# A mixture-of-experts decoder step: one weight transfer per expert instead of two, and the down product right behind its own activations

## The reference, cut to what matters

```python
def _swiglu(x, wg, wu, wd):
    return (jax.nn.silu(x @ wg) * (x @ wu)) @ wd

def block_fn(args):
    toks, e = args
    xb = xf[toks]
    return _swiglu(xb, w_gate[e], w_up[e], w_down[e])

yb = lax.map(block_fn, (row_tok.reshape(n_blocks, EXPERT_BLOCK), block_e))
return jax.ops.segment_sum(yb.reshape(R, D) * row_w[:, None], row_tok, num_segments=N)
```

## Time and profile before

| | us |
|---|---|
| median of 3 runs (lowest, highest) | 2084.97 (2083.36, 2092.01) |
| the profiled execution's own time | 2083.33 |
| its span, first to last instruction | 2081.7 |

### The profile page before, as it was taken

One profiled execution on the slowest core, in us unless ns is written; L12 is line 12 of the kernel. 1 busy time (PEld: TensorE's weight loads), 2 busy tenths in 40 slices (PEclk: granted clock), 3 DMA queues, 4 the chain that ended last, 5 costly groups with the idle time before them and its releaser, 6 DMA issues. The chain is left out here.

```text
span 2081.7 us, 34017 instructions
## 1 busy us (share of the span) xinstructions
PE 1714.9 (82%) x13065; PEld 1021.8 (49%) x13066; DVE 703.9 (34%) x1821; ACT 311.1 (15%) x665; POOL 355.2 (17%) x453
## 2 busy tenths in 40 slices
PE   5997988488889998785699988986688999987875
PEld 3455655244455454443355666654344555544432
DVE  0211235511413432231711265547312333331226
ACT  0221201110001111001002244331001111110110
POOL 3000100122212222221001011100122222222220
PEclk8999999699899999998789999998799999998997
DMA  9479874699999999994922599995499999999966
GB/s 329 169 264 348 313 303 138 268 416 425 393 383 370 421 418 407 401 401 180 350 105 71 189 291 329 326 343 216 195 423 420 397 409 403 421 411 401 402 278 227
DMA packets 132060, 674.14 MB, mean 324 GB/s; under 512 B 28111, under 2 KB 40527, under 8 KB 91620
## 3 DMA queue, kind: packets, MB, share of 16 engines
q1 hardware_dynamic: 84880, 570.20, 69.6%
q10 hardware_dynamic: 21604, 55.96, 8.0%
q0 software_dynamic: 25456, 46.27, 6.2%
HBM read 651.03 MB, written 46.94 MB: 335 GB/s over the span
## 5 line engine op out<-in xcount | busy, mean ns | idle before, releaser
L2323 PE MATMUL bank<-ring,work 128*64 128x256 f32 x4096 | 535.8, 420 | 145.6 <-DMA ring<-in_exp_w 143.2
L2323 PEld LDWEIGHTS bank<-ring,work 128*64 128x64 f32 x4096 | 341.7, 151 | 309.0 <-issue 130.6
L2051 PE MATMUL bank<-ring,uT 128*128 128x512 f32 (+1 forms) x896 | 253.7, 498 | 5.5 <-DVE u L1481 4.2
L2335 PE MATMUL bank<-ring,work 128*64 128x512 f32 x1032 | 249.9, 605 | 1.3 <-DVE work L1762 0.9
L811 POOL DMA_INDIRECT work<-u_d,work x128 | 130.6, 1021 | 641.7 <-DVE work L1728 352.7
L1728 DVE COPY work<-work 128x1 int32<-128x1 int32 (+1 forms) x128 | 19.2, 153 | 530.1 <-ACT work L1184 529.3
L2051 PEld LDWEIGHTS bank<-ring,uT 128*128 128x128 f32 (+1 forms) x896 | 117.6, 167 | 132.1 <-issue 112.0
L818 POOL DMA_INDIRECT pair_d<-work x128 | 132.6, 1036 | 268.1 <-DVE work L1732 255.1
L1184 ACT ACTIVATE work<-bank 128x128 f32<-128x128 f32 x128 | 35.5, 277 | 675.9 <-PE bank L2323 675.9
L1180 ACT COPY work<-bank 128x512 f32<-128x512 f32 x128 | 74.9, 585 | 292.8 <-PE bank L2335 292.8
L2315 PE MATMUL bank<-ident,work 128*128 128x128 f32 x516 | 97.5, 312 | 20.2 <-DMA work<-u_d,work 20.2
(11 more groups left out here) (363 smaller groups left out, 1735.9 us busy)
## 6 DMA issues: line engine op xcount, KB each, us to landing
ring<-in_exp_w SPq DMA_DIRECT2D x128, 2048.0 KB, 17.8
ring<-in_exp_w SPq DMA_DIRECT2D x128, 1024.0 KB, 13.0
ring<-in_ada_w SPq DMA_DIRECT2D x24, 2048.0 KB, 11.7
ring<-in_cache_k SPq DMA_DIRECT2D x128, 256.0 KB, 6.6
ring<-in_cache_v SPq DMA_DIRECT2D x128, 256.0 KB, 6.8
ring<-in_gla_w_in SPq DMA_DIRECT2D x6, 2048.0 KB, 18.1
ring<-in_kv_w_mod SPq DMA_DIRECT2D x4, 2048.0 KB, 11.7
work<-pair_d ACTq DMA_DIRECT2D x4, 2048.0 KB, 9.6
```

Source lines behind the costliest of these rows:

```text
L2051: ins = mm(out, uT[:, c, t0:t0 + r], ring_pair(unit)[:, c, cols], start=(c == 0), stop=(c == KT - 1), skip_group_check=(t == ST))
L2323: ins = mm(psum[s][64 * c:64 * c + 64, 0:2 * P].rearrange("p (a n) -> p a n", a=2), xT[:, s, j * P + 64 * half:j * P + 64 * half + 64], gu ...
L2335: ins = mm(psum[3 + s][64 * c:64 * c + 64, :], hT[:, s, 64 * f:64 * f + 64], w[:, f, c * 512:(c + 1) * 512], start=(f == 0), stop=(f == 1) ...
```

## The change

Each expert's 3 MB come as one transfer with runs of 24 KB in each partition, issued when the down product of expert e-3 is finished; one semaphore per slot tells of all three matrices. On TensorE the down product of expert e directly follows the transpose of its own hidden values, still behind the transposes of the rows of expert e+1. On DVE the copy of the hidden values goes ahead of the copy of the turned rows. On ACT the copy of the result of e-1 goes ahead of the `silu` of e. The separate down product behind the loop goes.

```diff
             def moe(l):
                 wr.at(0)
                 for e in range(NE):
-                    wr.take(("gate_up", l, e), 2, (h_full, NE * l + e + 1))
-                    wr.take(("down", l, e), 1, (y_full, NE * l + e + 1))
+                    wr.take(("expert", l, e), 3, (y_full, NE * l + e + 1))
...
             def load_expert(l, e, s):
 
-                sp.dma_start(ring[:, 3 * s:3 * s + 2, :].rearrange("p a n -> p (a n)"),
-                             W["exp_w"][l, ds(e, 1)].rearrange("o p n -> p (o n)")[:, 0:2 * UNIT])\
-                  .then_inc(unit_full[3 * s], 16)
-
-            def load_down(l, e, s):
-                sp.dma_start(ring[:, 3 * s + 2, :],
-                             W["exp_w"][l, ds(e, 1)].rearrange("o p n -> p (o n)")[:, 2 * UNIT:3 * UNIT])\
-                  .then_inc(unit_full[3 * s + 2], 16)
+                sp.dma_start(ring[:, 3 * s:3 * s + 3, :].rearrange("p a n -> p (a n)"),
+                             W["exp_w"][l, ds(e, 1)].rearrange("o p n -> p (o n)")).then_inc(unit_full[3 * s], 16)
 
             def load_experts(l):
                 for e in range(3):
-                    free_units(("gate_up", l, e))
+                    free_units(("expert", l, e))
                     load_expert(l, e, e)
-                    free_units(("down", l, e))
-                    load_down(l, e, e)
                 base = l * NE
                 load_shared(l)
 
                 def steady(e, s):
-                    sp.wait_ge(h_full, e + (base - 2))
+                    sp.wait_ge(y_full, e + (base - 2))
                     load_expert(l, e, s)
-                    sp.wait_ge(y_full, e + (base - 2))
-                    load_down(l, e, s)
...
                 def one(e, s, i, first=False):
+                    if not first:
+                        y_out(e - 1, (s + 2) % 3, stored_before(e - 1, (s + 2) % 3, i))
                     act.wait_ge(h_full, e + (base + 1))
                     act.activation(sil[:, s, :], psum[s][:, 0:P], ACT.Silu).then_inc(sem("sil_ready"), 1)
-                    if not first:
-                        y_out(e - 1, (s + 2) % 3, stored_before(e - 1, (s + 2) % 3, i))
...
                     tt(hs[:, s, :], sil[:, s, :], psum[s][:, P:2 * P], ALU.mult).then_inc(sem("h_ready"), 1)
+                    dve.wait_ge(sem("hT_full"), e + (base + 1))
+                    dve.tensor_copy(hT[:, s, :], psum[s][:, 2 * P:3 * P]).then_inc(sem("hT_ready"), 1)
                     if turn_next:
                         rows_turned(e + 1, (s + 1) % 3)
-                    dve.wait_ge(sem("hT_full"), e + (base + 1))
-                    dve.tensor_copy(hT[:, s, :], psum[s][:, 2 * P:3 * P]).then_inc(sem("hT_ready"), 1)
...
-                def one(e, s, i, first=False, fresh=False, last=False):
+                def one(e, s, i, fresh=False, last=False):
                     pe.wait_ge(sem("xT_ready"), e + (base + 1))
-                    pe.wait_ge(unit_full[3 * s], (i + loads[0][s]) * 16)
+                    pe.wait_ge(unit_full[3 * s], (i + loads[s]) * 16)
                     gu = ring[:, 3 * s:3 * s + 2, :].rearrange("p a (k n) -> p k a n", n=FE)
                     gate_up(s, gu, h_full)
                     if not last:
                         s1 = (s + 1) % 3
                         rows(e + 1, s1, i + (s + 1) // 3, fresh=fresh)
-                    if not first:
-                        s0 = (s + 2) % 3
-                        i0 = i if s else i - 1
-                        pe.wait_ge(unit_full[3 * s0 + 2], (i0 + loads[1][s0]) * 16)
-                        pe.wait_ge(sem("hT_ready"), e + base)
-                        down(s0, ring[:, 3 * s0 + 2, :].rearrange("p (f n) -> p f n", f=2), y_full)
                     pe.wait_ge(sem("h_ready"), e + (base + 1))
                     turn_hidden(s, sem("hT_full"))
+                    pe.wait_ge(sem("hT_ready"), e + (base + 1))
+                    down(s, ring[:, 3 * s + 2, :].rearrange("p (f n) -> p f n", f=2), y_full)
...
                 one(NE - 1, 0, NE // 3, last=True)
-                pe.wait_ge(unit_full[2], (NE // 3 + loads[1][0]) * 16)
-                pe.wait_ge(sem("hT_ready"), base + NE)
-                down(0, ring[:, 2, :].rearrange("p (f n) -> p f n", f=2), y_full)
```

More of the change, by code:

```diff
@@ L2341, in experts @@
                 base = l * NE
-                loads = [[wr.items[(kind, l, s)][1] for s in range(3)] for kind in ("gate_up", "down")]
+                loads = [wr.items[("expert", l, s)][1] for s in range(3)]
                 def rows(e, s, i, fresh=False):
@@ L2371, in experts @@
                 for e in range(3):
-                    one(e, e, 0, first=(e == 0), fresh=(e < 2))
+                    one(e, e, 0, fresh=(e < 2))
                 with pe.Fori(1, SHARED_FROM) as i:
```

## The result

| | us |
|---|---|
| before, median of 20 runs (lowest, highest) | 2084.19 (2077.83, 2094.19) |
| after, median of 20 runs (lowest, highest) | 2090.5 (2083.4, 2099.99) |
| ratio, with its 95% interval | 1.0031 (1.0016 to 1.0045) |
| after, the profiled execution and its span | 2089.25, 2087.6 |

The change costs 0.3%. That lies within the 0.5% I had called "same", and the time lies in my range, but it goes the other way than my -3.2 us, and the interval leaves no change out. I was 9.5 us too low. That the time still stands in the range is in part luck: what I had priced saved about what I had said, and a loss for which I had set nothing came on top.

What follows compares the result with a forecast made beforehand. The DMA engines were taken to bound the stages at 8.66 us an expert. Terms of -9.3, +1.3, +3.0 and +1.8 summed to -3.2 us, giving 2080.1 for the profiled execution and 2081.8 for the median; forecast 2081, range 2062 to 2112.

Steps and rivals of the forecast that it cites:

- no DMA time is left there: Middle of both layers' stages: DMA share 1.01 at 420 GB/s, so the DMA engines set 8.66 us an expert.
- TensorE's chain under cover: TensorE, per expert: chain grows 0.70 us to 7.11, hidden by the 2.2 us wait for weights; cost 0.
- The packets: Weight transfers: 9 fewer packets per DMA engine and expert at 8.5 ns each, 9.3 us saved.
- that upper price: Rival, weights' queue: packets cost more, 24 ns each, so 27 us saved instead of 9.3, 2064 us; chance 0.16.
- long packets that move worse: Rival, weight transfers: 24 KB runs take 0.41 us an expert more, 50 us lost, 2141 us; chance 0.06.
- The two ends: Start and end of each layer's stage: +1.3 and +3.0 us over both layers; layer 0's later overflow weights +1.8 once.
- The DMA engines don't run dry: Slot released 0.7 us later: loads in line still last until the next issue, even behind the shared expert; cost 0.
- the gathers become late: Rival: gathers behind doubled packets land at 13.3 us; over 15.8 us TensorE waits; at 16.5, 2128 us; chance 0.08.
- The slow clock: Rival, TensorE: gate and up products at half clock make its chain 8.80 us, +17 us, 2100; chance 0.07.
- The fixed cost of a transfer: Rival, weight transfers: merging saves fixed cost until TensorE's chain stops it at 189 us, 1896 us; chance 0.01.
- The change does what it says: Weight transfers: its opposite was a rival, the 24 KB run being cut up again, 2091 us; chance 0.02.
- My 123 us of idle time: Sign of being right: TensorE's idle time before gate and up products falls from 208 to near 123 us.

Runs made afterwards that it cites:

- the spread: Each expert's rows dealt evenly over the DMA engines: on the changed kernel 2061.74 us (0.9890), on order-alone 2046.96 us (0.9823), on the kernel before 2053.84 us (0.9860).
- order-alone: The changed kernel with its order and release, but each expert's weights as two transfers again, runs of 16 and 8 KB: 2083.1 us, ratio 0.9986.
- the 8 KB runs: The changed kernel's order with each expert's weights as three transfers of 8 KB per partition, all released together: 2091.54 us, ratio 1.0031.
- packed: The order-alone kernel with rows dealt so that 40 rows fill five of a half's eight DMA engines and leave three without any: 2098.91 us, ratio 1.0077.
- both indices early: The changed kernel with DVE writing the gather's index of e+4 and the scatter's index of e-1 earlier: 2081.92 us, ratio 0.9984; with rows spread too 2044.64 us, 0.9818.
- fewer requests: The changed kernel with each scatter replaced by a single row to a spare buffer, experts' sums missing from the output: 2048.92 us, ratio 0.9826.

## Why the prediction was wrong

**What bounded the kernel** was read from a mean. A share of 1.01 is a mean over 16 engines, and "no DMA time is left there" did not follow from it: the spread took some 30 us off at the same share. That the engines which carry most set the pace is the explanation that fits all the deals; no row shows one engine.

**TensorE's chain under cover, at 0:** right. An expert without a wait takes 6.87 us (I had 7.11 from the pieces), and the order-alone run, which has this chain and the later release, is at 0.9986. The steps from the transposes of the rows to the next expert's products confirm the pieces (answering to the earlier trace rows):

```profile
411.38 0.75 PE L2304 MATMUL bank<-ident,work 128*128 128x128 f32 x4
412.21 0.33 PE L2319 MATMUL bank<-ident,work 128*128 128x128 f32 x1
412.93 1.94 PE L2324 MATMUL bank<-ring,work 128*64 128x512 f32 x8 [0.38 <-DVE work L1749]
414.69 1.68 PE L2312 MATMUL bank<-ring,work 128*64 128x256 f32 x14
```

From the first of these to the down product it is 1.55 us (I had 0.84 + 0.80 = 1.64), and the step across the DVE copy is 0.72, not 0.80.

**The packets, at -9.3:** borne out in size. The packet count fell by 18,432 (132060 to 113628), as foretold. The weights' queue took 69.6% of 2081.7 us before and 68.8% of 2087.6 after, 12.6 us less; the 8 KB runs give 8.4 ns a packet where I had 8.5. That queue time is no clean price, since packed and spread, with equal packets, differ by some 25 us in it (69.6% of 2097.9 us, 70.2% of 2043.6). The ratios of the 8 KB and the order-alone run, 9.4 us apart give or take 6, are the firmer ground. At 24 ns a packet they would be 26 us apart, so that upper price is out, and so is the rival of long packets that move worse.

**The two ends, at +1.3 and +3.0 a pair, and +1.8 for the overflow weights:** small, and not tested by themselves. At the start of layer 0 SyncE's first issue comes 9.2 us after the first product (399.01 to 408.19), where I had 9.1. At its end (answering to the earlier trace rows) the last expert's products and its down product stand thus:

```profile
953.77 3.67 PE L2312 MATMUL bank<-ring,work 128*64 128x256 f32 x32
...
958.85 1.94 PE L2324 MATMUL bank<-ring,work 128*64 128x512 f32 x8 [0.38 <-DVE work L1749]
```

That is 7.0 us from start to end, where I had worked out 7.1.

**The step that failed** is "The DMA engines don't run dry, I take 0", together with the chance of 0.08 for *the gathers become late*. I had the mechanism, and its deciding point of 15.8 us, but two things in its price were wrong. I scaled the wait by the length of a packet and so put the landing at 13.3 us, with cover to spare; it was 15.2 in the median of the run, 16.0 and 17.3 in two stretches in full flow, right at that point. I had a row in hand that speaks for more: GpSimd's 2273 packets against 4282. Halving the second makes it 2141, fewer than GpSimd's, so by the theory of turns the line at GpSimd's queue grows, whatever one packet takes. And I asked only whether TensorE would wait, and not what stands behind that wait: the down product, the slot's release, ACT's copy behind a scatter, a bias on a third queue.

The sizes: order-alone is at 0.9986 and after at 1.0031, 9.4 us apart. The packets should have taken 9.3 off, so the late landings cost about 19 us, an estimate from medians of two comparisons, good to some 5 us, and with my price of the packets in it. Of that at most the 11.44 us at 860 us come from the single late bias load; how the rest divides between gathers, scatters and the slower clock behind them was not measured.

**The others.** The slow clock as a cause of its own is out: order-alone has it no more often than before (granted clock 0.98 and 0.98 in the stages, 0.93 and 0.94 before). The fixed cost of a transfer is out too: 122 transfers fewer gave nothing of the kind. (The section of the Trainium skill from which I took the 2.0 us, the anatomy of one DMA in "DMA: Bandwidth & Descriptors", describes transfers that GpSimd issues; these are SyncE's. Its advice to merge stands elsewhere on that page.) The change does what it says.

Of what I listed as a sign of being wrong, waits of the row transposes for the gather came true, 58 times, and the share fell to 0.94 from 800 to 920 us, around the bias load (1.00 before). Of the signs of being right, weights landed after 13.9 us (436 to 560 us) and not 18 to 19, and gathers after 15.2, not 9 to 14. My 123 us of idle time came from 208, which has the weight loads in it; from 143.2 it would have been some 58, and it was 19.3.

**Shown and not shown.** Shown: the loss comes with the 24 KB runs and not from the order; gathers are late with 24 KB runs and not with 16 + 8 or 8; an earlier issue lengthens them by about as much, and with both indices early the loss is gone; fewer requests, with fewer bytes, shorten them. Argued: how the 19 us divide, that the busiest engine explains the spread, and that an engine changes queue after each packet. No row shows a single turn; the Trainium skill ("DMA: Bandwidth & Descriptors", queues, rings and completion order) states it, and the landings in all these runs agree.

## What to carry to other kernels

Before merging transfers, count the packets of every queue that shares the DMA engines with them. Here the small stream's landings nearly doubled when the big one had fewer packets than it (1866 beside 2085 in 110 us), and stayed as they were with 3802. Issuing the small stream's requests earlier is mostly taken back by longer landings; it gave 0.5 to 0.7% here, and nothing where the landings were short. The saving of a merge here is only about 8.4 ns a packet; a mean DMA share of 1.0 does not say that there is nothing left. Ask which engine carries what: dealing rows evenly over the partitions gave 1.4 to 1.6%, more than any choice of run length.

## What had not been expected of the hardware

- Runs of 24 KB went as single packets (2049 packets for 44.85 MB), and with them a gather's median landing was 15.2 us, where it was 8.1 before, 8.0 with 16 + 8 KB and 6.8 with 8 KB runs in the same order.
- A bias load of 0.5 MB on ACT's queue, the last of four loads issued there together, landed about 41 us after its issue, from 814.42 to 856.03, beside 24 KB runs. In the kernel before, that queue's last packet ended some 27 us after the same issue, and DVE had no wait for it in the kernels with 16 + 8 or 8 KB.
- Kernels that differ only in the partitions of an expert's rows moved 400 and 420 GB/s from 800 to 920 us at a DMA share of 1.00 and 1.01, and 413 and 424 from 1515 to 1640 us at 1.01.
